# Key-choosing attention on Trainium2: the longest tile goes first, its keys are chosen in the stage in front

## What is computed

```python
# recurrent branch (6 heads of 64): token shift on its columns, then normalised keys
z = z + (prev_row(z) - z) * mu                  # columns r, k, v, g, low
kk = k * k_k
kk = kk / max(norm(kk, per head), 1e-12)

# key-choosing attention (4 heads of 64), rows in 8 blocks ("tiles") of 128
sc = relu(iq @ ik.T / sqrt(32)) * iw, summed over 8 heads, causal
idx = top_k(sc, 256)                            # 256 keys for each row
att = softmax(q @ k[idx].T / 8); out = att @ v[idx] * silu(g)
```

## Time and profile before

| | us |
|---|---|
| median of 3 runs | 4011.86 (4009.95 to 4012.99) |
| profiled execution, its own time | 4015.7 |
| its span, first to last instruction | 4014.4 |
| TensorE busy | 3644.9 (91%) |
| VectorE busy | 2205.6 (55%) |
| ScalarE busy | 1133.7 (28%) |
| GpSimd busy | 506.2 (13%) |

### The profile page before, as it was taken

The page is one execution under the profiler, slowest core; times in us unless marked ns, Lnnn a source line. Parts: engine busy times, 40 slices in busy tenths (PEclk is TensorE's granted clock), DMA queues, the critical chain, the costliest instruction groups (busy, mean ns, idle before and its releaser), DMA issues. The chain is left out here.

```text
span 4014.4 us, 58104 instructions
## 1 busy us (share of the span) xinstructions
PE 3644.9 (91%) x22944; PEld 2327.5 (58%) x22944; DVE 2205.6 (55%) x4609; ACT 1133.7 (28%) x2429; POOL 506.2 (13%) x314
## 2 busy tenths in 40 slices
PE   5999848799999997999997997998999988898898
PEld 4555424685478544656665885444655655787444
DVE  3143476446764573589865553342389875653343
ACT  2121135221122011411134555222320114555222
POOL 0010033000110010012211111110002211121110
PEclk7999969899999998999998998999999999998899
DMA  6332322323433452123331204111013341202220
GB/s 216 137 115 88 109 101 79 116 95 147 177 117 105 147 185 86 32 63 93 111 108 50 72 20 164 49 65 57 27 56 92 105 137 52 59 30 102 94 77 23
DMA packets 234283, 377.16 MB, mean 94 GB/s; under 512 B 30742, under 2 KB 163870, under 8 KB 233014
## 3 DMA queue, kind: packets, MB, share of 16 engines
q1 hardware_dynamic: 234030, 373.58, 28.2%
HBM read 290.84 MB, written 69.08 MB: 90 GB/s over the span
## 5 line engine op out<-in xcount | busy, mean ns | idle before, releaser
L3413 PE MATMUL win_acc<-across_room,across_hT 128*128 128x384 f32 (+3 forms) x3072 | 907.8, 456 | 3.7 <-PEq L83 3.7
L3413 PEld LDWEIGHTS win_acc<-across_room,across_hT 128*128 128x128 f32 x3072 | 561.0, 191 | 345.1 <-issue 15.0
L2480 DVE TENSOR_SCALAR_CACHE_REDUCE win_rl<-d_sc,win_mid 128x384 f32<-128x384 f32 (+5 forms) x384 | 363.2, 946 | 35.9 <-DVE win_mid L2488 24.0
L3252 PE MATMUL tail_wo<-tail_w_out,across_room 128*128 128x512 f32 x512 | 230.1, 604 | 9.3 <-issue 9.3
L453 PE MATMUL zin_acc<-zin_wt,across_hT 128*128 128x512 f32 (+2 forms) x640 | 229.2, 513 | 0.0
L3263 PE MATMUL tail_wg<-tail_w_gate,across_room 128*128 128x512 f32 x512 | 225.3, 594 | 1.0 <-DVE across_room L3093 1.0
L3474 ACT ACTIVATE d_ot<-win_acc 128x384 f32<-128x384 f32 (+1 forms) x144 | 66.9, 466 | 562.8 <-PE win_acc L3413 562.7
L453 PEld LDWEIGHTS zin_acc<-zin_wt,across_hT 128*128 128x128 f32 x640 | 119.9, 190 | 98.3 <-issue 88.6
L3252 PEld LDWEIGHTS tail_wo<-tail_w_out,across_room 128*128 128x128 f32 x512 | 98.0, 194 | 129.0 <-issue 129.0
L1700 PE MATMUL mlp_bk<-across_hT,across_room 128*128 128x256 f32 x768 | 171.0, 379 | 0.0
L3263 PEld LDWEIGHTS tail_wg<-tail_w_gate,across_room 128*128 128x128 f32 x512 | 96.5, 191 | 116.5 <-issue 116.5
(11 more groups left out here) (492 smaller groups left out, 6869.3 us busy)
## 6 DMA issues: line engine op xcount, KB each, us to landing
across_room<-in_w SPq DMA_DIRECT2D x96, 1024.0 KB, 6.9
across_room<-in_w_in SPq DMA_DIRECT2D x18, 1536.0 KB, 8.3
s_z<-d_ot SPq DMA_DIRECT2D x14, 1536.0 KB, 6.5
across_room<-in_w_ada SPq DMA_DIRECT2D x8, 2048.0 KB
across_hT<-s_z SPq DMA_DIRECT2D x16, 832.0 KB, 5.7
win_zp<-d_ot SPq DMA_DIRECT2D x8, 1344.0 KB
front_w<-in_w_ada SPq DMA_DIRECT2D x4, 2048.0 KB, 15.7
zin_wt<-in_w_in SPq DMA_DIRECT2D x4, 2048.0 KB, 9.2
```

What stands on the lines that cost most here:

```text
L2480: s(dve.tensor_scalar(junk[:, q % 2, 0:L], sc[q][:, :], mid[:, q:q + 1], 0.0, ALU.is_gt, ALU.add, accum_out=cnt[:, q:q + 1]))
L3252: mm = pe.matmul(wo[:, c, :], yT[:, n % 2, q, :], W["out"][:, q, c * COL:(c + 1) * COL], start=q == 0, stop=q == KC - 1)
L3413: mm = pe.matmul(acc[:, u % RING, 0:w], hT[:, k, t * P:(t + 1) * P], wt[:, i % 2, k, 0:w], start=k == 0, stop=k == KC - 1)
```

## The change

The chunk k moves from the eleventh place to the fifth, where v was, v to the tenth and r behind it. GpSimd now shifts k, g, low and v, VectorE shifts r behind the bisection. The product `kk` = k * `k_k` goes to GpSimd, behind k's shift, and the squares with their sums go to ScalarE (`norms`: 48 operations of 64 columns behind the copies of the second chunk after k, which is g), so that VectorE keeps only maximum, reciprocal and the last product. SP waits for the squares (`n6_ready`) before it fetches g's rows into `zp`, since the squares are written there, and for `kk_raw` before it stores k.

The choosing becomes a function, `choose_keys`. It is called for tile 7 at the end of the projection, on VectorE between r's shift and the end of the key norm; GpSimd fills `ones` early in the stage and makes tile 7's mask at its end. `TILE_ORDER` becomes 7, 6, 5, 1, 4, 0, 3, 2, the other five tiles are chosen one step behind each head from the first on, and `keep_busy` is gone. A few buffers move in `room` and `early`.

```diff
-TILE_ORDER = list(range(T0)) + list(range(NT - 1, T0 - 1, -1))
+TILE_ORDER = [7, 6, 5, 1, 4, 0, 3, 2]
+CHOSEN_ORDER = [t for t in TILE_ORDER if t >= T0]
+def choosing_buffers(room):
+    return room[:, 0:SEQ], room[:, SEQ:2 * SEQ], room[:, 2 * SEQ:3 * SEQ], room[:, 8064:8064 + SEQ], room[:, 9344:9344 + SEQ]
+
+def choose_keys(s, dve, x, lo, hi, g, p_, cand, ones, need, chosen, n):
+    w = x.shape[-1]
+    s(dve.tensor_scalar(g, x[:, :], hi, 0.0, ALU.is_gt, ALU.add, accum_out=need))
+    s(dve.tensor_scalar(need, need, -1.0, float(TOPK), ALU.mult, ALU.add))
+    yield
+    s(dve.scalar_tensor_tensor(cand[:, 0:w], x[:, :], lo, g, ALU.is_gt, ALU.subtract))
+    yield
+    s(dve.tensor_tensor_scan(p_, ones[:, 0:w], cand[:, 0:w], 0.0, ALU.mult, ALU.add))
+    yield
+    dve.scalar_tensor_tensor(p_, p_, need, cand[:, 0:w], ALU.is_le, ALU.mult).then_inc(chosen, 1)
+    dve.wait_ge(chosen, START + n)
+    yield
 ...
                 scores(0)
                 scores(1)
-                keep_busy(0, 16)
 ...
                         if k >= 1:
                             values(k - 1)
-                            if groups[k - 1][0] != m:
-                                busy_after(m - 1)
 ...
                 for m in range(NM):
                     i, h = m // DSA_H, m % DSA_H
                     attend(m)
-                    if not (i == 1 and h < 2):
-                        next(steps, None)
+                    next(steps, None)
 ...
-WIN_CHUNKS = [("idx", ...), ("qkv", ...), ("dg", ...), ("", DIL0, 384), ("v", 2 * RW, RW), ("", DIL0 + 384, 384),
-              ("g", 3 * RW, RW), ("", DIL0 + 768, 384), ("low", 4 * RW, P), ("r", 0, RW), ("k", RW, RW), ("gate", DIL0 + 1152, 384)]
+WIN_CHUNKS = [("idx", ...), ("qkv", ...), ("dg", ...), ("", DIL0, 384), ("k", RW, RW), ("", DIL0 + 384, 384),
+              ("g", 3 * RW, RW), ("", DIL0 + 768, 384), ("low", 4 * RW, P), ("v", 2 * RW, RW), ("r", 0, RW), ("gate", DIL0 + 1152, 384)]
 ...
+                        if q == 1:
+                            sp.wait_ge(n6_ready, START + 1)
                         sp.dma_start(zp[1:113, :, 0:w], ot[0:112, j, :, 0:w]).then_inc(zp_in, DMA)
 ...
+                        if i == K:
+                            sp.wait_ge(kk_raw, START + 1)
 ...
+                def norms(t):
+                    for h in range(RWH):
+                        c = slice(h * HD, (h + 1) * HD)
+                        ins = act.activation(zp[:, t, c], kk[:, t, c], ACT.Square, accum_out=n6[:, t, h:h + 1])
+                    if t == NT - 1:
+                        ins.then_inc(n6_ready, 1)
 ...
+                        if i == K + 2 and t >= 1:
+                            act.wait_ge(kk_raw, START + 1)
+                            norms(t - 1)
+                            if t == NT - 1:
+                                norms(t)
 ...
             def _(gp):
+                gp.wait_ge(roped, START + 2)
+                gp.memset(ones, 1.0)
                 gp.wait_ge(mu_in, START + (len(order) + 1) * DMA)
                 for i in order[:ON_POOL]:
                     shift(gp, i, gstep, 0, g_shifted)
+                    if i == K:
+                        gp.wait_ge(g_shifted, START + 1)
+                        gp.tensor_tensor(kk[:, :, :], ot[:, slot(K), :, 0:RW], bc_mid(k_k, NT), ALU.mult).then_inc(kk_raw, 1)
+                gp.wait_ge(L["first_chosen"], START + 1)
+                gp.tensor_tensor(mask0, pre0, gt0, ALU.add).then_inc(L["first_step"], 1)
+                gp.wait_ge(L["first_step"], START + 1)
+                gp.tensor_scalar(mask0, mask0, -1.0, BIG, ALU.add, ALU.mult).then_inc(L["first_mask"], 1)
 ...
-                shift(dve, K, dstep, ON_POOL, d_shifted)
-                dve.wait_ge(d_shifted, START + 1)
-                dve.tensor_tensor(kk[:, :, :], ot[:, slot(K), :, 0:RW], bc_mid(k_k[:, :], NT), ALU.mult).then_inc(dstep, 1)
-                dve.wait_ge(dstep, START + 3)
-                dve.tensor_tensor(zp[:, :, :], kk[:, :, :], kk[:, :, :], ALU.mult).then_inc(dstep, 1)
-                dve.wait_ge(dstep, START + 4)
-                dve.tensor_reduce(n6[:, :, :], by_head(zp[:, :, :]), X, ALU.add).then_inc(n6_ready, 1)
+                shift(dve, R, dstep, ON_POOL, d_shifted)
+                for _ in choose_keys(s, dve, sc[NT - 1 - T0], ..., gt0, pre0, cand, ones, need, L["first_chosen"], 1):
+                    pass
                 dve.wait_ge(root, START + 1)
```

More of the change, by code:

```diff
@@ L2502, in dsa_attend @@
         ident, causal = L_["ident"], B["causal"]
-        gt, pre, mask = (carve(room, q * 2 * SEQ, [2, SEQ]) for q in range(3))
-        cand, ones = room[:, 6 * SEQ:7 * SEQ], room[:, 7 * SEQ:8 * SEQ]
+        gt0, pre0, cand, ones, mask0 = choosing_buffers(room)
+        gt, pre, mask = ([first, room[:, (3 + q) * SEQ:(4 + q) * SEQ]] for q, first in enumerate((gt0, pre0, mask0)))
         need = ph.sb("need", [P, 1])
@@ L2512, in dsa_attend @@
         po = ph.ps("po", [P, 2, 512])
-        ones_set, step, gstep, made, masked, expd, turned, pT_ready, o_made, inv_ready, o_read, row_done, chosen, mask_ready = (
-            ph.sem(n) for n in ("ones_set step gstep made masked expd turned pT_ready o_made inv_ready o_read row_done chosen "
+        step, gstep, made, masked, expd, turned, pT_ready, o_made, inv_ready, o_read, row_done, chosen, mask_ready = (
+            ph.sem(n) for n in ("step gstep made masked expd turned pT_ready o_made inv_ready o_read row_done chosen "
                                 "mask_ready").split())
@@ L2541, in _ @@
             def _(pe):
-                def keep_busy(j, n):
-                    for _ in range(n):
-                        pe.matmul(po[:, j, 256:512], B["v"][:, 0:2, :].rearrange("p b c -> p (b c)"), B["g"][:, 0, :], start=True, stop=True)
                 def scores(m):
@@ L2576, in values @@
                         mm.then_inc(o_made, 1)
-                def busy_after(m):
-                    i, h = m // DSA_H, m % DSA_H
-                    if i < 2 and h < DSA_H - 1:
-                        keep_busy(i % 2, 8 if m == 2 * DSA_H - 2 else 2)
                 scores(0)
                 scores(1)
-                keep_busy(0, 16)
                 k = 0
@@ L2606, in s @@
                     gp.wait_ge(gstep, START + count[0])
-                gp.memset(ones[:, :], 1.0).then_inc(ones_set, 1)
                 for i, t in enumerate(TILE_ORDER):
+                    if i == 0:
+                        continue
                     L, j = (t + 1) * P, i % 2
-                    mk = mask[:, j, :]
+                    mk = mask[j]
                     if i >= 2:
@@ L2652, in attend @@
                     L = (TILE_ORDER[i] + 1) * P
-                    dve.wait_ge(mask_ready, START + i + 1)
+                    if i == 0:
+                        dve.wait_ge(L_["first_mask"], START + 1)
+                    else:
+                        dve.wait_ge(mask_ready, START + i)
                     dve.wait_ge(made, START + m + 1)
@@ L2671, in rows_out @@
                                       B["g"][:, TILE_ORDER[i], :], ALU.mult).then_inc(row_done, 1)
-                dve.wait_ge(ones_set, START + 1)
-                steps = chain.from_iterable(choose(i) for i in range(T0, NT))
+                steps = chain.from_iterable(choose(q) for q in range(1, NS))
                 for m in range(NM):
@@ L3311, in win2 @@
     NCH, LOCAL, RING = len(CHUNKS), 3, 3
-    SHIFTED = ("v", "g", "low", "r", "k")
     ON_POOL = 4
-    order = [i for i, c in enumerate(CHUNKS) if c[0] in SHIFTED]
+    order = [i for i, c in enumerate(CHUNKS) if c[0] in ("v", "g", "low", "r", "k")]
     shapes = [i for i in order if CHUNKS[i][0] in ("g", "low")]
@@ L3323, in win2 @@
         tmp, cs = carve(room, 8064, [4, NT * 40]), carve(room, 9344, [NT, 2, 12])
-        n6, k_k = carve(room, 9536, [NT, RWH]), room[:, 9584:9584 + RW]
+        n6, k_k = carve(early, 2048, [NT, RWH]), early[:, 2096:2096 + RW]
+        need = early[:, 2480:2481]
+        gt0, pre0, cand, ones, mask0 = choosing_buffers(room)
         ikd, kd = carve(early, 0, [NT, 4, IDX_D]), carve(early, 1024, [NT, 2, HD])
```

51 lines of the change are left out of this document (21 added, 30 removed).

## The result

The changed kernel takes 4126.49 us (median; 4123.18 to 4130.51) beside 4010.9 for the kernel before: **1.029 times as long**, 95% interval 1.0272 to 1.0308. That is 116 us more where 12 less were forecast, and outside the range. Its profiled execution spans 4124.8 us against 4014.4, 110.4 more; TensorE's mean granted clock is 0.918 against 0.953.

What follows compares the result with a forecast made beforehand. VectorE's queue was taken to end the projection in both layers, TensorE being busy for most of both stages. Projection +9.0 and attention -21.0 gave -12.0 us, from 4011.86 to 4000; range 3987 to 4010.

Steps and rivals of the forecast that it cites:

- the attention's term: Attention with the longest tile first: 99.7 us to VectorE's last operation instead of 110.2, -10.5 per layer, bounds -12.5 and -7.
- the filling: Filling matmuls removed from the attention: less 3 of their 3.67 us, since part of them hid a wait.
- Rival D: Attention without filling matmuls: the clock falls inside it, 27 us at half clock per layer, 4027 us in all; chance 0.08.
- the first score row: Attention's start: the longest tile's first score row taken at 3.8 us instead of 21.8.
- GpSimd's product: Bisection in the projection: VectorE is held for the whole product behind k's shift, +6.7 us per layer; other bound +0.
- rival B: GpSimd's new operations, product and mask, cost VectorE nothing: 3983 us; chance 0.12.
- Phases: Bisection: GpSimd's shifts cost VectorE 16.5 us each, 3.5 for the 128-wide one; phases alone worth 4 us either way.
- The chain: VectorE's work behind the bisection up to the attention: 24.5 us against 26.7, -2.2 per layer, including +1.8 from GpSimd's mask.
- Seam: Between projection and attention: TensorE idle about 12 us in both layers instead of 5.1 and 10.3.
- The stage in front: Projection: +7.0 us in the first layer and +2.0 in the second, together +9.0.
- ScalarE's norms: Projection: squares with sums on ScalarE, 3 us a tile beside 5.2 us on TensorE, so covered.
- the 128-column chunk: Projection's chunk after the norms: 0 to 2 us of TensorE waiting for ScalarE, costing nothing while VectorE ends the stage.

Runs made afterwards that it cites:

- a_fillmid: Changed kernel with 16 filling matmuls at the attention's start and 2 behind each of the first three heads of its fourth to sixth tile: 4014.4 us, ratio 1.0003.
- a_seam: Changed kernel with 12 and 30 filling matmuls at the end of the projection, none in the attention: 4069.3 us.
- a_late16: Changed kernel with 16 filling matmuls behind the scores of head 12, in mid-attention, none at the start: 4102.4 us.
- b_nofill: Kernel before the change without any of its filling matmuls, everything else as it was: 4074.5 us.
- a_ord2: Changed kernel, tile order 7, 6, 1, 5, 0, 4, 3, 2; 8 and 14 fillings ending the projection, 4 in the attention, first mask made there: 4129.7 us.
- a_d4: Changed kernel, tiles 7 down to 0, two more early choosing steps, 4 filling matmuls at the attention's start, none before it: 4133.0 us.
- a_seam2: Changed kernel, tiles 7 down to 0, 8 and 14 filling matmuls at the end of the projection, none in the attention: 4129.1 us.
- a_best1: Changed kernel, tiles 7 down to 0, 8 and 14 fillings ending the projection, 4 in the attention, first mask moved into the attention: 4132.0 us.
- a_fill16: Changed kernel with only 16 filling matmuls put back behind the first two heads' scores: 4034.7 us, ratio 1.0055.

## Why the prediction was wrong

1. **The step that failed is the attention's term (-10.5 per layer): it took TensorE to be at full clock from the first microseconds on.** The sum took every duration at full clock but for 1.1 us and booked the filling as a gain ("less 3 of the 3.67 us and some more of filling matmuls that lie inside"), work without a use. With the clock lost the attention is 166.9 us, where the forecast was 99.7 to VectorE's last operation plus some 3.5 to the next stage, which is 103.2. The forecast priced the filling at 3 us, and it was worth some 63. With the clock kept by 8 fillings the attention is 102.6 and 103.6 us. That this meets the forecast is in part luck: these runs have another tile order, two more early choosing steps and 3.8 us of filling. In the forecast's own order the clock was kept to the end only with 34 fillings a layer (a_fillmid), at 109.8 and 109.6.
2. **Rival D had the mechanism, the place and the sign, but 0.08 of the chance and a price of 27 us.** Its evidence against was read wrongly: "the stage's later heads, which had no filling, stood at full clock to its end". The earlier trace rows show a clock that was up and stayed up over small gaps; they say nothing of whether it comes up, or survives a wait of 1.4 to 2.5 us. The same stage of the kernel before gives the missing row: without its fillings, in its second layer, 157 us at 0.50. Its price was bounded at "27 us of it"; nothing in the profile put an end to the stretch, and it was some 160 us in each layer: 166.9 instead of 103.2, 64 us a layer.
3. **What the prediction itself showed and didn't use**: at full clock the longest tile's first head passes through VectorE and ScalarE before TensorE has the next thing to do. The prediction has the first score row at 3.8 us, and the scores of head 2 wait for it. In the kernel before, 9 us of filling stood at this place (behind the first two heads' scores, at half clock to begin with):

```profile
2045.61 9.03 PE L2544 MATMUL datt_po<-d_g,d_v 128*128 128x256 f32 x32
```

4. **GpSimd's product: +6.7, measured +6.9 and +6.2** in the round of k's shift (31.85 and 30.29 us against 24.91 and 24.12), and 6.3 and 6.5 where it was removed. Right, rival B is out.
5. **Phases: forecast +2.5 and -2.5 beside the product, measured +0.6 and -0.4** by lost time (58.1 and 60.4 us in all against the forecast 59.7, before 50.5 and 54.6, the last by that layer's own round of 7.76). The bisection was +7.6 and +9.0 instead of +9.2 and +4.2, the second because all its rounds were longer.
6. **The chain: 24.1 and 24.2 us, forecast 24.5.** The 1.8 us came another way: VectorE's last product didn't start late (0.7 behind the choice), it was stretched by 1.5, and GpSimd's second operation from 1.04 to 4.02.
7. **Seam: TensorE idle 10.1 and 16.6 us, forecast some 12 in both.** ScalarE's norms were covered, and TensorE had no wait in the 128-column chunk, as the lower bound had it. The stage in front cost 5.0 and 6.4 us, 11.4 together, where 9.0 were forecast: of this half nearly the size was right, and the mechanism but for the way in which the mask costs (point 6).

The Trainium skill ("TensorE: Matmul & The Clock Gate", Part 1) says that an idle array drops to half clock and that activity releases it. The fall behind waits of 1.42 to 2.46 us and the rise in a dense stretch agree in kind. But here an array that the profile shows busy for 50.00 of 50.00 us stayed at 0.50.

**Open**: why the heads of this kernel, without a gap, don't lift the clock in most attentions and do so in three (25, 37 and 39 us in: a_seam, a_late16, b_nofill, each in its first layer), is not shown; nor whether it is the covered waits or the filling's own work that keeps the clock at the start; nor whether a single short tile between two long ones is borne (a_ord2 didn't reach it).

## What to carry to other kernels

Before filling work is taken out, or a stage's order changed, ask of each stretch not only what TensorE waits for but at what clock it comes out of that wait: this stage took 167 us at half clock and 103 with the clock kept, and a full clock in the rows of before is evidence only for the work that stands there now. Filling belongs where the first items run through the other engines and TensorE would wait for them: with 8 matmuls of 256 columns there the attention took 103 us, with 4 it took 169, and with 16 it took 104 to 107. And a helper engine that holds the bound engine can cost its full duration, as here: the same product was cheaper on VectorE itself, put where the operand is just ready.

## What the runs showed of the hardware

- A granted clock of 0.50 lasted through 157 us in which TensorE was busy for 156. Busy by the profile doesn't mean at full clock.
- Among the first heads the clock fell behind a wait of 1.42 us (the changed kernel), 1.41 (a_seam, first layer), 2.03 (a_d4), and 2.46 with a shorter one in front (a_seam2, a_best1, a_ord2); and later behind a stretch of 8 us with 6.58 busy (a_fill16). It was kept over waits of 0.25 and 0.30 us, in a_seam's second layer over 1.40 and 1.27, and in the kernel before over a stretch with 9.02 of 10 us busy.
- Between two rounds of the bisection, at the loop's jump, VectorE has nothing for 0.37 us in the first layer of both kernels, and in the second for 0.40 before and 0.51 after the change. Over 32 rounds (7.76 and 7.87 us) that is 3.5 us, for code that wasn't touched; with the loop in two pieces the round was 7.76 again. What makes the difference was not tried.
